# Expert rows on TensorE: none while cache pages are worked on, every fourth afterwards; gates and V rows two slots later

## The chip, the cores and the metric

The kernel runs on one core of one Trainium2 chip. The metric is device time in microseconds (us) of one execution; lower is better. The program is one launch with a fixed instruction stream for each engine (TensorE = PE, VectorE = DVE, ScalarE = ACT, GpSimd = POOL, SyncE = SP) and semaphores between them.

## What is computed

One inference step of a decoder layer for a prompt of 512 tokens and 8 sample tokens. The part that matters here is the last of the program:

```python
# 8 sequences attend over 16 cache pages of 128 tokens each
ckv_all = concatenate([cache_ckv[pages], ckv_i]); k = mla_keys(ckv_all, kpe_all, w_uk, g_k)
o = softmax(q . k) @ ckv_all @ w_uv                       # mla_sample, one sequence at a time
# expert layer, for blocks of 128 tokens, 8 heads x 16 chosen experts = 128 per token
ids, g = top-k of product keys, softmax                   # peer_ffn
act = gelu(einsum('thkd,td->thk', u_tab[ids], hb))
out = einsum('thkd,thk->td', v_tab[ids], g * act)
```

`u_tab` and `v_tab` have 16384 rows of 1024 fp32. All arithmetic is fp32.

## The kernel before

The program has a front (projections, convolution, scan, prompt attention, merge) that the change does not touch, and then `experts`, where the expert layer of the prompt, the page attention of the samples, and the rest of the samples are laid into one order of **slots**. Slot x (0 to 511 for the prompt: 4 tiles of 128 tokens, 128 slots each; 512 to 519 for the samples) stands for one chosen expert of each of 128 tokens. Each engine has its own loop `for x in range(...)` over the slots with what it does in slot x; the loops are tied by semaphores alone.

For the row of a slot the work is:
- POOL issues an indirect DMA that gathers 128 U rows (512 KB) into `u[:, x % UR]` (`UR` = 4 buffers, L2070), and an indirect DMA for the 128 V rows of slot x - BEHIND into `v[:, y % VR]` (`VR` = 8 buffers, L2077). Before each it waits until the buffer's last user is done (`u_used`, `v_used`).
- DVE multiplies and sums the U rows with the tokens' vectors (L2655), which gives one number per token in `dots`.
- Every `GS` = 4 slots ACT applies Gelu (L2386) and DVE multiplies by the gate (L2668, after waiting for `gelued`): that is the coefficient `coef`.
- Row x - LAG is added: on DVE as one `scalar_tensor_tensor` acc += v * coef (`add`, L2555; the first of a tile is L2551), or, where `by_pe(x)`, on PE: ACT makes a diagonal matrix of the coefficients (`diag`, L2394) and PE multiplies it with the V rows into `psV` (`expert_row`, L2179, four matmul records per row). `finish` adds `psV` to `acc` (L2562), multiplies by the gate of the block and adds to the residual.

Before the change `by_pe(x)` holds for every eighth slot from 62 on (x % 8 == 3): 56 rows on PE, 456 on DVE.

Into slots 62 to 435 the 128 cache pages are spread, one every 2.94 slots (`page_slot`). For a page PE transposes it (`turn`, L2148, L2149), and multiplies it with `wx` in three banks (`page_bank`, L2164, L2166); ACT copies (`page_copy`) and takes squares and sums of the keys (`page_squares`, L2377). After the 16 pages of a sequence (47 slots) a chain over DVE, ACT and PE makes the softmax and the weighted sum (`ending`, L2578 to L2602 on DVE, L2218 and L2219 on PE, slots `end` to `end` + 19). SP loads pages into 24 buffers. Buffers come free when a sequence's weighted sum is done (`weighed`). DVE also does the search for the experts of later tokens in parts between the rows (`search_part`, L1764 to L1808). From `TAIL` = slot 460 on, the samples' own projections, their expert search (slot 497 on) and their 8 expert slots follow.

The order of the work within an engine is the order of its loop. In ACT's loop, Gelu of slots 4g to 4g + 3 stands in slot 4g + 3, behind the squares of the pages of the slots before; DVE wants it in slot 4g + 5. PE does the row of slot y in its slot y + 5.

Of the kernel before, what the change touches and what calls it, by code (L numbers as in the profile page):

```python
# [19 lines left out]
ALU = mybir.AluOpType  # L20
# [10 lines left out]
TT = TP // P  # L31
# [12 lines left out]
SL = PH * TK  # L44
# [1683 lines left out]
GS = 4  # L1728
UR, VR, NPG = 4, 8, 24
LAG, BEHIND = 6, 2  # L1730
PAGE_LAG = 5
FIRST_PAGE, PAGE_SPAN = 62, 376
PE_EVERY = 8
UNITS, PARTS = TT * PH, 16
NSLOT, EXTRA = TT * SL, TK // 2
# [5 lines left out]
def after(eng, sem, n):  # L1741
    if n > 0:
        eng.wait_ge(sem, n)
# [67 lines left out]
def experts(nc, A, K, L, parts, shared, D_, outs):  # L1811


    with ExitStack() as ctx:
# [24 lines left out]
        v, u = m.sb("v", [P, VR, D]), m.sb("u", [P, UR, D])  # L1839
# [101 lines left out]
        by_pe = lambda x: x >= FIRST_PAGE and x % PE_EVERY == 3  # L1941
        on_pe = [x for x in range(NSLOT) if by_pe(x)]
        pe_index = {x: d for d, x in enumerate(on_pe)}
        last_on_pe = [max(x for x in on_pe if x // SL == t) for t in range(TT)]
        first_on_pe = [min(x for x in on_pe if x // SL == t) for t in range(TT)]
# [134 lines left out]
        def _(pe):  # L2080
# [89 lines left out]
            def expert_row(x):  # L2170
                t, r = x // SL, x % VR
                pe.wait_ge(v_in[r], 16 * (x // VR + 1))
                if x < NSLOT:
                    d = pe_index[x]
                    pe.wait_ge(diag_made, d + 1)
                    if x == first_on_pe[t]:
                        after(pe, acc_merged, t)
                    for c in range(2):
                        last = pe.matmul(psV[:, c, :], diag[:, d % 2, :], v[:, r, c * 512:(c + 1) * 512], start=(x == first_on_pe[t]),  # L2179
                                         stop=(x == last_on_pe[t]))  # L2180
# [20 lines left out]
            for x in range(XEND):  # L2201
# [25 lines left out]
                if NSLOT <= x - LAG < NSLOT + EXTRA:  # L2227
                    expert_row(x - LAG)
# [86 lines left out]
        def _(act):  # L2315
# [66 lines left out]
            for x in range(XEND):  # L2382
# [4 lines left out]
                if x - 3 >= 0 and x - 3 in pe_index:  # L2387
                    y = x - 3
                    d = pe_index[y]
                    act.wait_ge(weighted, y // GS + 1)  # L2390
                    if d >= 2:
                        o = on_pe[d - 2]
                        act.wait_ge(v_used[o % VR], o // VR + 1)
                    act.activation(diag[:, d % 2, :], K["ident"][:, :], ACT.Copy, scale=coef[:, y // SL % 2, y % SL:y % SL + 1]).then_inc(diag_made, 1)  # L2394
# [103 lines left out]
        def _(dve):  # L2498
# [58 lines left out]
            def finish(t):  # L2557
# [3 lines left out]
                dve.wait_ge(v_used[last_on_pe[t] % VR], last_on_pe[t] // VR + 1)  # L2561
                dve.tensor_tensor(acc[:, :], acc[:, :], psV[:, :, :].rearrange("p c n -> p (c n)"), ALU.add).then_inc(acc_merged, 1)  # L2562
                dve.wait_ge(acc_merged, t + 1)
# [4 lines left out]
            for x in range(XEND):  # L2568
# [92 lines left out]
                if x >= GS + 1 and (x - GS - 1) % GS == 0:  # L2661
                    g = (x - GS - 1) // GS
# [145 lines left out]
```

## Time and profile before

| | |
|---|---|
| time, three runs | 2823.23, 2823.42, 2836.57 us (median 2823.42) |
| the profiled execution's own time | 2826.46 us |
| its span, first to last instruction | 2824.8 us |
| busy in the span | PE 85%, DVE 75%, POOL 51%, ACT 33% |
| moved by DMA | 776.5 MB, mean 275 GB/s |
| granted TensorE clock, mean | 0.916 |

The span has a front of some 1069 us, the first slots to 1292 us, the stretch with the pages to about 2520 us, and the rest. A share over the whole span mixes these, so the rows below are taken from one stretch at a time. "Busy" leaves out register, semaphore and DMA-issuing instructions of SP and ACT; POOL's indirect DMA instructions count, with a gap of 0.30 us before each that is called "issue". A wait is put down to the releaser that came last. In the pages' stretch the rows of L2655 count the slots.

### The profile page before, as it was taken

The numbers are of one execution on the slowest core, as the hardware profiler recorded it, in microseconds if no ns is written. First come the engines' busy times: TensorE is split into PE (matmuls) and PEld (weight loads), VectorE is DVE, ScalarE is ACT, GpSimd is POOL, SyncE is SP. The second block draws the span as 40 slices with busy tenths as digits, with TensorE's granted clock in tenths as the row PEclk, the third lists the DMA queues.
The fourth block names the chain that finished last, engine by engine and source line by source line (L and its number), as shares of the span: only waits on it lengthen the run. The fifth ranks groups of instructions, "written<-read, shape, count | busy, mean of one in ns | idle before, by whom it ended". The sixth has DMA issues, their size and how long they took to land.

```text
span 2824.8 us, 37378 instructions
## 1 busy us (share of the span) xinstructions
PE 2394.0 (85%) x11945; PEld 1655.2 (59%) x11945; DVE 2106.2 (75%) x4074; ACT 927.2 (33%) x3628; POOL 1442.1 (51%) x1207
## 2 busy tenths in 40 slices
PE   5999997978989986887999999999999989974343
PEld 3999997864448853444565656565656546542120
DVE  3675887965555228897888978888888879897777
ACT  3431102224251112223453535444444535430110
POOL 1121332210001105776777767777778767775575
PEclk7999998989899998998999999999999999995665
DMA  6334776544006768999989999999989899999997
GB/s 196 90 80 139 212 219 151 125 129 140 12 16 211 211 223 318 399 393 388 359 282 387 361 369 351 343 362 330 391 299 397 301 372 347 356 358 357 399 337 288
DMA packets 384017, 776.51 MB, mean 275 GB/s; under 512 B 49033, under 2 KB 198618, under 8 KB 383785
## 3 DMA queue, kind: packets, MB, share of 16 engines
q0 software_dynamic: 155568, 566.17, 54.1%
q1 hardware_dynamic: 206970, 183.33, 20.8%
q10 hardware_dynamic: 21284, 24.63, 3.0%
q8 instruction: 95, 1.56, 0.2%
q14 instruction: 100, 0.82, 0.1%
HBM read 744.85 MB, written 29.37 MB: 274 GB/s over the span
## 4 chain that ended last, share of the span: by engine, by line
PE 23%; issue 12%; another core or an unknown queue 8%; DMA 8%; DVE 5%; POOL 3%; SPq 3%; ACT 1%; POOLq 0%; DVEq 0%; ACTq 0%
PE mix_pair L2164 16%; DMA mix_u<-in_peer_u,mix_ids 6%; DVE mix_acc L2555 2%; DVE mix_u L2655 2%; POOL mix_v L2077 2%; PE mix_pair L2087 2%; PE mix_pair L2179 1%; POOL mix_u L2070 1%; SPq L2027 1%; PE mix_pair L2148 1%; DMA pag_kpe<-in_cache_kpe 1%; SPq L2026 1%; PE mix_pair L2116 1%; PE mix_pair L2166 1%
## 5 line engine op out<-in xcount | busy, mean ns | idle before, releaser
L2164 PE MATMUL mix_pair<-pag_wx,pag_ckvT 128*128 128x384 f32 (+3 forms) x3072 | 972.9, 464 | 24.1 <-issue 13.5
L2077 POOL DMA_INDIRECT mix_v<-in_peer_v,mix_ids x512 | 640.2, 1250 | 225.4 <-issue 164.4
L2164 PEld LDWEIGHTS mix_pair<-pag_wx,pag_ckvT 128*128 128x128 f32 x3072 | 569.7, 193 | 315.9 <-issue 47.6
L2070 POOL DMA_INDIRECT mix_u<-in_peer_u,mix_ids x512 | 602.3, 1176 | 295.2 <-issue 144.0
L2655 DVE CUSTOM_DVE_ANT_0 mix_u<-mix_u,mix_h 128x1024 f32<-128x1024 f32 x512 | 624.2, 1219 | 165.0 <-DMA mix_u<-in_peer_u,mix_ids 142.9
L2555 DVE SCALAR_TENSOR_TENSOR mix_acc<-mix_v,mix_coef,mix_acc 128x1024 f32<-128x1024 f32 x452 | 579.5, 1282 | 0.0
L2377 ACT ACTIVATE mix_pair<-mix_pair 128x128 f32<-128x128 f32 x1024 | 270.8, 264 | 450.7 <-PE mix_pair L2164 276.4
L386 POOL CAST inp_w_hi<-inp_w 128x1024 fp32r<-128x1024 f32 x73 | 111.1, 1522 | 375.5 <-DMA inp_w<-in_w_in 296.2
L2377 ACT ACTIVATION_READ_ACCUMULATOR mix_pair<-mix_pair 128x1 f32 x1024 | 192.9, 188 | 0.0
L386 POOL CAST mrg_w_hi<-mrg_w 128x1024 fp32r<-128x1024 f32 x24 | 29.0, 1209 | 304.7 <-DMA mrg_w<-in_w_br_a 271.1
L2179 PE MATMUL mix_pair<-mix_v,mix_diag 128*128 128x512 f32 x224 | 115.3, 640 | 68.1 <-ACT mix_diag L2394 42.8
L352 PE MATMUL stp_ps<-inp_h_hi,inp_w_hi 128*128 128x260 f32 x512 | 148.3, 290 | 15.3 <-DVE inp_w_lo L346 9.6
L354 PE MATMUL stp_ps<-inp_h_hi,inp_w_lo 128*128 128x260 f32 x512 | 146.5, 286 | 0.0
L353 PE MATMUL stp_ps<-inp_h_lo,inp_w_hi 128*128 128x260 f32 x512 | 146.2, 286 | 0.0
L2365 ACT ACTIVATE pag_ckvT<-mix_pair 128x512 f32<-128x512 f32 x128 | 75.8, 592 | 149.9 <-DMA scn_ce<-keep_acs 56.7
L2386 ACT ACTIVATE mix_coef<-mix_dots 128x4 f32<-128x4 f32 x128 | 26.0, 203 | 295.4 <-DVE mix_dots L2655 257.0
L2116 PE MATMUL mix_pair<-chs_h2T,chs_wq 128*128 128x512 f32 (+2 forms) x352 | 117.2, 492 | 0.9 <-ACT chs_h2T L2349 0.6
L352 PE MATMUL cnv_ps<-inp_h_hi,inp_w_hi 128*128 128x260 f32 x400 | 116.3, 291 | 0.0
L354 PE MATMUL cnv_ps<-inp_h_hi,inp_w_lo 128*128 128x260 f32 x400 | 114.1, 285 | 0.0
L353 PE MATMUL cnv_ps<-inp_h_lo,inp_w_hi 128*128 128x260 f32 x400 | 113.9, 285 | 0.0
L2179 PEld LDWEIGHTS mix_pair<-mix_v,mix_diag 128*128 128x128 f32 x224 | 43.9, 202 | 113.2 <-issue 60.1
L352 PEld LDWEIGHTS stp_ps<-inp_h_hi,inp_w_hi 128*128 128x128 f32 x512 | 98.5, 192 | 17.0 <-issue 9.4
(532 smaller groups left out, 4328.4 us busy)
## 6 DMA issues: line engine op xcount, KB each, us to landing
inp_w<-in_w_in SPq DMA_DIRECT2D x72, 512.0 KB, 5.0
pag_ckv<-in_cache_ckv SPq DMA_DIRECT2D x88, 256.0 KB
mrg_w_ada<-in_w_ada SPq DMA_DIRECT2D x16, 1024.0 KB, 5.4
chs_wq<-in_peer_wq SPq DMA_DIRECT2D x11, 1024.0 KB
all_shared<-in_cache_ckv SPq DMA_DIRECT2D x40, 256.0 KB
keep_proj<-stp_out ACTq DMA_DIRECT2D x32, 260.0 KB
ada_w_ada<-in_w_ada SPq DMA_DIRECT2D x4, 2048.0 KB, 9.8
stp_st<-in_state_ssm POOLq DMA_DIRECT2D x8, 1024.0 KB, 7.2
```

Source lines behind the costliest of these rows:

```text
L352: pe.matmul(out, w_hi, x_hi, start=first, stop=False)
L353: pe.matmul(out, w_hi, x_lo, start=False, stop=False)
L354: return pe.matmul(out, w_lo, x_hi, start=False, stop=last)
L386: pool.tensor_copy(self.hi[:, c % 4], self.w[:, c % 2]).then_inc(self.rounded, 1)
L2070: pool.indirect_dma_start(u[:, x % UR, :], None, u_rows, bass.IndirectOffsetOnAxis(at, 0)).then_inc(u_in[x % UR], 16)
L2077: pool.indirect_dma_start(v[:, y % VR, :], None, v_rows, bass.IndirectOffsetOnAxis(at, 0)).then_inc(v_in[y % VR], 16)
L2116: last = pe.matmul(bank[2 + side][:, 0:w], wq[:, n % 2, k, side * P:(side + 1) * P], h2T[:, k, cols], start=(k == 0), stop=(k == KD - 1))
L2164: last = pe.matmul(to, ckvT[:, g % 2, k, :], wx[:, k, lo:hi], start=(k == 0), stop=(k == KL - 1))
L2179: last = pe.matmul(psV[:, c, :], diag[:, d % 2, :], v[:, r, c * 512:(c + 1) * 512], start=(x == first_on_pe[t]), stop=(x == last_on_pe[t]))
L2377: last = act.activation(psN[j][:, at:at + NOPE], psN[j][:, at:at + NOPE], ACT.Square, accum_out=ss[:, b % 2, t, h:h + 1])
L2555: dve.scalar_tensor_tensor(acc[:, :], v[:, r, :], c, acc[:, :], ALU.mult, ALU.add).then_inc(v_used[r], 1)
L2655: dve.tensor_tensor_reduce(u[:, r, :], u[:, r, :], h2[:, t % 2, :], 1.0, 0.0, ALU.mult, ALU.add, dots[:, t % 2, slot:slot + 1]).then_inc(u ...
```

## The change

Rows go to PE only from slot `end[-1]` = 440 on, the end of the pages, and there every fourth (x % 4 == 3): 18 rows (443 to 511). The 47 rows from slot 67 to 435 that PE had are DVE's. Tiles 0 to 2 then have no row on PE, so `finish` adds `psV` only for tile 3. `LAG` goes from 6 to 8 and `BEHIND` from 2 to 4: a V row is loaded two slots later and added two slots later. The gate multiplication on DVE stands in slot 4g + 7, where it stood in 4g + 5; ACT's diagonal in slot y + 5, where it stood in y + 3; PE's row in slot y + 7. The samples' rows stay at their slots on PE.

```diff
@@ constants @@
-LAG, BEHIND = 6, 2
+LAG, BEHIND = 8, 4
-PE_EVERY = 8
+PE_EVERY = 4
@@ experts @@
-        by_pe = lambda x: x >= FIRST_PAGE and x % PE_EVERY == 3
+        by_pe = lambda x: x >= end[-1] and x % PE_EVERY == 3
         on_pe = [x for x in range(NSLOT) if by_pe(x)]
         pe_index = {x: d for d, x in enumerate(on_pe)}
-        last_on_pe = [max(x for x in on_pe if x // SL == t) for t in range(TT)]
-        first_on_pe = [min(x for x in on_pe if x // SL == t) for t in range(TT)]
+        of_tile = [[x for x in on_pe if x // SL == t] for t in range(TT)]
+        merged_by = [sum(1 for rows_ in of_tile[:t] if rows_) for t in range(TT + 1)]
@@ tensor @@
-                if NSLOT <= x - LAG < NSLOT + EXTRA:
-                    expert_row(x - LAG)
+                if NSLOT <= x - LAG + 2 < NSLOT + EXTRA:
+                    expert_row(x - LAG + 2)
@@ scalar @@
-                if x - 3 >= 0 and x - 3 in pe_index:
-                    y = x - 3
+                if x - 5 >= 0 and x - 5 in pe_index:
+                    y = x - 5
@@ vector @@
-                dve.wait_ge(v_used[last_on_pe[t] % VR], last_on_pe[t] // VR + 1)
-                dve.tensor_tensor(acc[:, :], acc[:, :], psV[:, :, :].rearrange("p c n -> p (c n)"), ALU.add).then_inc(acc_merged, 1)
-                dve.wait_ge(acc_merged, t + 1)
+                if of_tile[t]:
+                    row = of_tile[t][-1]
+                    dve.wait_ge(v_used[row % VR], row // VR + 1)
+                    dve.tensor_tensor(acc[:, :], acc[:, :], psV[:, :, :].rearrange("p c n -> p (c n)"), ALU.add).then_inc(acc_merged, 1)
+                    dve.wait_ge(acc_merged, merged_by[t + 1])
-                if x >= GS + 1 and (x - GS - 1) % GS == 0:
-                    g = (x - GS - 1) // GS
+                if x >= GS + 3 and (x - GS - 3) % GS == 0:
+                    g = (x - GS - 3) // GS
```

## Rows read from the trace of the kernel before

**Rows 1.** Windows view: us, busy time and instructions by engine, PEclk, DMA share, GB/s.

```profile
1069.00:1292.00 223.00, 160.64 (x497) 87.28 (x496) 195.41 (x382) 47.98 (x97) 161.76 (x134) 0.86 1.01 384
1292.00:2520.00 1228.00, 1170.44 (x4445) 730.39 (x4444) 1032.99 (x2078) 568.78 (x2943) 901.93 (x741) 0.98 0.96 353
2520.00:2825.00 305.00, 117.80 (x454) 56.79 (x452) 233.27 (x441) 39.52 (x104) 193.32 (x163) 0.64 0.92 345
...
1145.50:1271.00 125.50, 109.33 (x354) 61.81 (x354) 115.37 (x226) 24.63 (x57) 99.35 (x80) 0.93 1.03 395
```

**Rows 2.** Chain of waits, 1327 to 1400: start, us, what.

```profile
1354.86 6.48 PE mix_pair L2164 x22
...
1362.86 6.48 PE mix_pair L2164 x22
1369.34 1.72 PE mix_pair L2179 x4
...
1372.58 6.48 PE mix_pair L2164 x22
```

**Rows 3.** Groups by line, 1292 to 2520: PE's expert rows, then DVE's.

```profile
L2179 PE MATMUL mix_pair<-mix_v,mix_diag 128*128 128x512 f32 x184 | 86.8, 594 | 0.7 <-issue 0.7
...
L2655 DVE CUSTOM_DVE_ANT_0 mix_u<-mix_u,mix_h 128x1024 f32<-128x1024 f32 x371 | 451.9, 1218 | 97.5 <-DMA mix_u<-in_peer_u,mix_ids 77.5 <-issue 18.5
L2555 DVE SCALAR_TENSOR_TENSOR mix_acc<-mix_v,mix_coef,mix_acc 128x1024 f32<-128x1024 f32 x323 | 414.2, 1282 | 0.0
...
L2668 DVE TENSOR_TENSOR mix_coef<-mix_coef,mix_gate 128x4 f32<-128x4 f32 x93 | 14.9, 161 | 69.0 <-ACT mix_coef L2386 57.4 <-issue 11.4
L2581 DVE RECIPROCAL mix_rstd<-mix_rstd 128x128 f32<-128x128 f32 x7 | 6.7, 953 | 22.9 <-ACT mix_rstd L2424 13.4 <-issue 9.5
L2562 DVE TENSOR_TENSOR mix_acc<-mix_acc,mix_pair 128x1024 f32<-128x1024 f32 x3 | 3.7, 1221 | 0.1
```

**Rows 4.** Waits of DVE, PE and POOL, 1292 to 2520: us, times, longest.

```profile
DVE mix_u L2655 <- DMA mix_u<-in_peer_u,mix_ids: 77.5, 82, 3.2
DVE mix_coef L2668 <- ACT mix_coef L2386: 57.4, 11, 8.6
DVE mix_u L2655 <- issue: 18.5, 29, 1.9
...
PE mix_pair L2148 <- DMA pag_kpe<-in_cache_kpe: 13.3, 2, 11.1
...
POOL mix_u L2070 <- DVE mix_dots L2655: 37.4, 15, 4.3
POOL mix_v L2077 <- DVE mix_acc L2555: 25.0, 4, 7.5
POOL mix_v L2077 <- PE mix_pair L2179: 21.0, 6, 13.4
```

**Rows 5.** Groups of POOL, 1292 to 2520, and last 1145.5 to 1271.

```profile
L2077 POOL DMA_INDIRECT mix_v<-in_peer_v,mix_ids x371 | 462.3, 1246 | 176.5 <-issue 119.9 <-DVE mix_acc L2555 25.0 <-PE mix_pair L2179 21.0
L2070 POOL DMA_INDIRECT mix_u<-in_peer_u,mix_ids x371 | 440.6, 1188 | 151.1 <-issue 108.7 <-DVE mix_dots L2655 37.4 <-DVE mix_acc L2551 5.1
...
L2077 POOL DMA_INDIRECT mix_v<-in_peer_v,mix_ids x40 | 60.2, 1506 | 14.3 <-issue 14.3
```

**Rows 6.** Timeline at 1158 to 1162 and at 1538: start, us, instruction, idle before.

```profile
1158.09 1.23 DVE L2655 CUSTOM_DVE_ANT_0 mix_u<-mix_u,mix_h 128x1024 f32<-128x1024 f32 x1 [0.58 <-DMA mix_u<-in_peer_u,mix_ids]
1158.28 1.85 POOL L2077 DMA_INDIRECT mix_v<-in_peer_v,mix_ids  x1 [0.30 <-issue]
...
1160.44 0.95 POOL L2070 DMA_INDIRECT mix_u<-in_peer_u,mix_ids  x1 [0.30 <-issue]
...
1161.69 1.83 POOL L2077 DMA_INDIRECT mix_v<-in_peer_v,mix_ids  x1 [0.30 <-issue]
...
1538.39 1.32 DVE L2555 SCALAR_TENSOR_TENSOR mix_acc<-mix_v,mix_coef,mix_acc 128x1024 f32<-128x1024 f32 x1
1538.45 0.95 POOL L2077 DMA_INDIRECT mix_v<-in_peer_v,mix_ids  x1 [0.30 <-issue]
```

**Rows 7.** After 2520: PE's expert rows, a DVE wait, the window 2740 to 2805.

```profile
L2179 PE MATMUL mix_pair<-mix_v,mix_diag 128*128 128x512 f32 x40 | 28.5, 851 | 67.4 <-ACT mix_diag L2394 42.8 <-DMA mix_v<-in_peer_v,mix_ids 24.6
...
DVE mix_v L1764 <- issue: 4.0, 1, 4.0
...
2740.00:2805.00 65.00, 8.91 (x10) 2.60 (x11) 55.95 (x108) 5.10 (x12) 47.02 (x42) 0.50 0.94 349
```

More of the change, by code:

```diff
@@ L2175, in expert_row @@
                     pe.wait_ge(diag_made, d + 1)
-                    if x == first_on_pe[t]:
-                        after(pe, acc_merged, t)
+                    if x == of_tile[t][0]:
+                        after(pe, acc_merged, merged_by[t])
                     for c in range(2):
-                        last = pe.matmul(psV[:, c, :], diag[:, d % 2, :], v[:, r, c * 512:(c + 1) * 512], start=(x == first_on_pe[t]),
-                                         stop=(x == last_on_pe[t]))
+                        last = pe.matmul(psV[:, c, :], diag[:, d % 2, :], v[:, r, c * 512:(c + 1) * 512], start=(x == of_tile[t][0]),
+                                         stop=(x == of_tile[t][-1]))
                 else:
```

## Prediction, made before the changed kernel was run

> **What bounds the kernel now.** I read the windows view first, to cut the span into stretches [rows 1]. The reader is to see that between 1292 and 2520 us, where the pages are, PE is busy 1170.4 of 1228 us (95%) at a granted clock of 0.98, while DVE is busy 1033.0 (84%) and DMA moves 353 GB/s. In the stretch just before it (1145.5 to 1271: no pages, no expert row on PE) DMA moves 395 GB/s and DVE is busy 92%. So with pages PE is what fills up first. After 2520 PE is nearly idle at a clock of 0.64. Second, the chain of waits inside the pages' stretch [rows 2]: from one page's block of 22 records to the next it is 8.00 us on PE, and 9.72 us where an expert row lies between, so a row costs PE 1.72 us in full. Third, the groups and waits of DVE [rows 3, 4]: of its 195 us of idle time 97.5 lie before L2655 (U rows not landed), 69.0 before the gate L2668 (Gelu late on ACT, which stands behind the squares of PE's pages), and 28.5 are the rest, of which 22.9 at the sequences' ends (L2581). Last, POOL [rows 5, 6].
>
> The stretch holds 371 rows, so a slot takes 1228 / 371 = 3.31 us. The sum is made for this stretch by DVE's time line, since DVE does every U row and releases POOL's buffers: its busy time plus its waits is the stretch's length.
>
> **The change part by part.**
>
> Rows taken from PE in the stretch: 184 records are 46 rows [rows 3], 46 x 1.72 = 79 us. PE's busy time falls to 1170.4 - 79 = 1091, with its present idle time of 57.6 us 1149 us. That is what PE would allow. It is a ceiling of the gain, 79 us, not the gain.
>
> Rows given to DVE: 46 x 1.282 us (L2555) = +59.0 us. `finish` loses three additions of `psV`, 3 x 1.22 = -3.7 us [rows 3]. The diagonals leave ACT, which has room (569 of 1228 us busy) [rows 1], at no gain. DVE's busy time becomes 1033.0 + 59.0 - 3.7 = 1088.3 us.
>
> Gates two slots later: the wait of 69.0 us has 11 cases put down to ACT, the longest 8.6 us [rows 4]. Two slots are 2 x 3.31 = 6.6 us, so at most 2.0 us of a case would be left, and PE is also less behind. With all 14 cases at that (three more are in the group's "issue" part) 28 us stay, with none 0. I take 10 us, nearer to none, because the mean case (69.0 / 14 = 4.9 us) is below 6.6. What is late next is the landing of U rows.
>
> Landings: 97.5 us now, in 111 waits (82 + 29) [rows 4]. An addition that DVE does while it would have waited costs nothing. Bounds: none of the 59.0 us hidden so, or all. By number 111 of 371 rows wait, which gives 18 us. As a wait in one slot also hides work of the slot before it, I take 27 us: 70.5 us are left.
>
> The rest of the waits, 28.5 us, is the chain at a sequence's end, where DVE, ACT and PE are tied with two slots between steps. The change leaves that, so I keep it whole.
>
> V rows issued and used two slots later: the distance from issue to use (LAG - BEHIND = 4 slots) and from use to the next issue into the same buffer stay, so 0. POOL's V row goes behind a later U row in its queue, and nothing else is on that queue. POOL no longer waits in the stretch for PE to release a V buffer (21.0 us in 6 waits, the longest 13.4 [rows 4]). That is what "unpaced" means here; its worth is inside the DVE sum, since DVE meets it as a late landing. Pages on SP keep their condition (`weighed`). PE waits 13.3 us for pages [rows 4], and if it gets there sooner that grows; PE has 1149 against the sum below, so up to some 45 us of it is hidden.
>
> Sum for the stretch: 1088.3 + 10 + 70.5 + 28.5 = 1197.3 us, against 1228: **-31 us**. PE (1149) fits below it. The nearest rows for rows without PE and pages say the same order: 40 rows in 125.5 us are 3.14 us each [rows 1, 5], with a background of other loads; 371 x 3.14 = 1165 us.
>
> After 2520: PE has 40 records = 10 rows now [rows 7], and will have the 18 of slots 443 to 511 (one of the 10 is slot 435's). DVE gives up 9 rows, 9 x 1.28 = 11.5 us, in a stretch of 305 us where it is busy 233 [rows 1]. Most of it is not DVE's to save. From 2740 to 2805 it is (56.0 of 65 us busy [rows 7]): there PE takes four rows where it had two, -2.6 us. Against it, PE does a further row ahead of the samples' scores, some 3.4 us (851 ns a record now, four records), and DVE already waits 4.0 us for these scores at L1764 [rows 7]. The end itself: the last V row waits for slot 519 of DVE where it waited for 517, but DVE's work up to there is the same sum of work minus the rows that PE takes, and PE's eight sample rows still run last. From -12 to +6 us; I take **-2 us**.
>
> Before 1292: adds start two slots later, and the same work is done by the same time: 0.
>
> In all -33 us on the profiled execution of 2826.5 us, 2793.5. Its time is 3.0 us above the median of the runs, so 2790.7, say **2791 us** on the median's scale.
>
> **A rule against the change.** POOL's V instruction takes 1.85 us when it begins under L2655 and ends 0.81 us after it, and 0.95 us otherwise [rows 6]: GpSimd is held while DVE reads two tensors. An instruction begun under L2555, which also reads two (v and acc), takes 0.95 us [rows 6]. The Trainium skill, SBUF — State Buffer, section "SBUF: two separate sides", has the shared port as an exclusive lock that a DVE instruction with two SBUF inputs takes against a GpSimd instruction that reads SBUF. For L2655 the trace agrees; for L2555 it doesn't. By the rule each of the 46 new additions would hold POOL for 0.9 us as well, 41 us in all; by the row 0.
>
> **The rivals.**
>
> Slower: **POOL's rhythm takes PE's place.** When POOL is behind, its V instruction always falls under L2655: 0.95 + 0.30 + 1.85 + 0.30 = 3.40 us a slot, which is the distance from 1158.28 to 1161.69 [rows 6]. Now POOL's mean is (462.3 + 440.6) / 371 + 0.60 = 3.03 us [rows 5], because DVE's and PE's holds let it get ahead again and its instructions then begin after L2655. If with no PE row left nothing resets it, each slot takes 3.40: 371 x 3.40 = 1261 us, +33, in all 2823 + 33 - 2 = 2854. It decides as soon as more than 6 of 10 slots run so. For it: 1145.5 to 1271 has a V mean of 1506 ns and no POOL wait but issue [rows 5]. Against it: even there a slot took 3.14.
>
> No change: **DVE takes PE's place.** The landings are set by rate and arrive later in step, none of the 59.0 us is hidden: 1088.3 + 10 + 97.5 + 28.5 = 1224 us, -4, with the end 2817. For it: DVE would be at 89% busy, and it was 92% in the densest stretch without PE rows [rows 1]. Against: 111 waits for landings are there to be filled. A bound by bytes would end here too: 353 GB/s x 1228 us = 433.5 MB. At the 395 GB/s of [rows 1] they need 1097 us and bind nothing. The Trainium skill, same page, section "A bandwidth-pool intuition that's wrong", has about 358 GB/s from HBM to a core. By that estimate the stretch couldn't fall below 1211 us, and the time below 2804; the trace's 384 and 395 speak against it.
>
> Faster yet: **all four are near 1100 and smooth each other.** The stretch runs like the one before the pages, 1165 us: -63, with the end 2758.
>
> The change might not do what it says: PE's rows may have cost it nothing since pages wait anyway. The 9.72 against 8.00 of [rows 2] excludes it.
>
> **How the numbers follow.** Forecast 2791 (its own range 2770 to 2809): 0.42. Faster yet (2758): 0.17. No change (2817): 0.24. POOL's rhythm (2854, in part 2835): 0.17. What a measurement of this kernel can tell from no change is about 0.5%, 14 us: faster is below 2809, slower above 2838. Faster 0.42 + 0.17 and a little of the third, 0.60; same 0.24; slower 0.16. The range leaves out half of the fastest case and the worse half of the slowest: 2750 to 2845.
>
> **What the changed kernel's profile would show.** In the pages' stretch: no L2179; L2555 at 1.28 us with about 46 more; PE busy near 1091 and no longer the fullest by far; DVE near 1088 of about 1197; the idle time before L2668 down from 69 to about 10; before L2655 about 70; no POOL wait for PE. If DVE's wait for landings rises above 110 with L2077's mean above 1.4 us, the slower rival holds. If the wait at L2668 stays above 40, the two slots were no cure. If PE's wait for pages passes 50 us, the step on SP's pages was wrong.

## The result

The changed kernel took **2863.6 us** (median of four runs, 2860.5 to 2874.7) beside 2830.0 us for the kernel before on the same chip: ratio **1.0132**, 95% interval 1.0084 to 1.0180. I had forecast 2791 us, with a range of 2750 to 2845. The time is slower than the forecast by 73 us and outside the range; the case "slower by over 0.5%", to which I had given 0.16, came true. Ratios, here and below, leave out executions over 1.5% above the fastest of the same kernel; medians are of all executions.

The profiled execution took 2865.5 us, its span is 2863.8 us. The stretch with the pages ends at 2549 instead of 2520 us. The windows view of after, with the columns of [rows 1]:

```profile
1292.00:2549.00 1257.00, 1121.08 (x4249) 705.78 (x4248) 1080.61 (x2122) 547.80 (x2886) 909.78 (x745) 0.94 0.93 346
2549.00:2863.00 314.00, 150.78 (x491) 64.39 (x489) 224.41 (x429) 42.45 (x118) 191.95 (x162) 0.64 0.89 332
```

The first line answers to the 1228 us of [rows 1], and holds 371 rows too. PE lost 49 us of busy time, where 79 were taken off it, and its granted clock fell from 0.98 to 0.94. DVE gained 48 us. DMA moved 346 instead of 353 GB/s. No engine is as full as PE was: PE is busy 89%, DVE 86%, and the stretch is 29 us longer. So the time is in waits, and the next views are those of DVE, whose busy time and waits make up the stretch. Groups of after by line, then DVE's waits (us, times, longest), both from 1292 to 2549:

```profile
L2657 DVE CUSTOM_DVE_ANT_0 mix_u<-mix_u,mix_h 128x1024 f32<-128x1024 f32 x371 | 450.7, 1215 | 77.7 <-DMA mix_u<-in_peer_u,mix_ids 60.0 <-issue 17.1
L2555 DVE SCALAR_TENSOR_TENSOR mix_acc<-mix_v,mix_coef,mix_acc 128x1024 f32<-128x1024 f32 x369 | 472.1, 1280 | 0.0
L2670 DVE TENSOR_TENSOR mix_coef<-mix_coef,mix_gate 128x4 f32<-128x4 f32 x93 | 14.6, 157 | 18.7 <-ACT mix_coef L2386 18.7
L2583 DVE RECIPROCAL mix_rstd<-mix_rstd 128x128 f32<-128x128 f32 x7 | 6.7, 953 | 24.9 <-ACT mix_rstd L2424 21.6 <-issue 3.3
L2077 POOL DMA_INDIRECT mix_v<-in_peer_v,mix_ids x373 | 495.4, 1328 | 144.5 <-issue 127.0 <-DVE mix_acc L2555 17.5
```

```profile
DVE mix_total L1806 <- ACT mix_exps L2433: 19.9, 4, 6.0
DVE mix_rstd L2580 <- ACT mix_raw L2379: 8.9, 1, 8.9
DVE all_o_lat L2604 <- PE mix_pair L2223: 8.5, 2, 5.3
DVE mix_rstd L2580 <- ACT mix_pair L2377: 8.0, 2, 5.5
```

(Lines moved by two: L2657, L2670, L2580, L2583 and L2604 of after are L2655, L2668, L2578, L2581 and L2602 of before.) Beside [rows 3]: landings fell from 97.5 to 77.7 us, the gate's wait from 69.0 to 18.7. What is left is 1257 - 1080.6 - 77.7 - 18.7 = **80.0 us, where there were 28.5**. It lies at the sequences' ends (L2580, L2583, L2604) and in the expert search at L1806, a line that had no such wait before: at all these places DVE stands for ACT or PE.

PE's waits in the same stretch of after:

```profile
PE mix_pair L2164 <- issue: 52.2, 19, 9.0
PE mix_pair L2164 <- ACT mix_raw L2379: 20.1, 8, 5.3
PE mix_pair L2148 <- DMA pag_kpe<-in_cache_kpe: 17.6, 4, 11.0
```

Before, the first of these was 13.5 us in 8 cases. PE does not wait for pages more (17.6 against 13.3 in [rows 4]); it stands inside a page's block.

None of the signs that I had named for the slower case shows: landings are below 110 us, the mean of L2077 is 1328 ns and below 1.4 us, the gate's wait is below 40 us, the wait for pages below 50. The time of that rival (2854) is near the measured one, its mechanism isn't what happened. That the two numbers are near is chance.

### The profile page after: what moved, and what is told of

Its sections match the earlier page's. It is cut to its first block, busy times and chain, and to the rows that moved or that the text cites. A ratio compares the mean times of both kernels' runs of the same rounds, so it can differ in the third digit from the quotient of the medians.

```text
span 2863.8 us, 37030 instructions
## 1 busy us (share of the span) xinstructions
PE 2375.3 (83%) x11793; PEld 1639.8 (57%) x11793; DVE 2147.4 (75%) x4109; ACT 909.9 (32%) x3590; POOL 1447.3 (51%) x1207
## 4 chain that ended last, share of the span: by engine, by line
PE 18%; issue 15%; DVE 10%; DMA 8%; another core or an unknown queue 4%; ACT 3%; POOL 3%; SPq 2%; POOLq 0%; DVEq 0%; ACTq 0%
PE mix_pair L2164 13%; DMA mix_u<-in_peer_u,mix_ids 5%; DVE mix_acc L2555 4%; DVE mix_u L2657 4%; POOL mix_v L2077 2%; ACT mix_pair L2377 1%; DMA all_shared<-in_peer_keys 1%; POOL mix_u L2070 1%; SPq L2027 1%; PE mix_pair L2148 1%; PE mix_pair L2087 1%; PE mix_pair L2116 1%; PE mix_pair L2250 1%; SPq L2026 1%
## 5 line engine op out<-in xcount | busy, mean ns | idle before, releaser
L2164 PE MATMUL mix_pair<-pag_wx,pag_ckvT 128*128 128x384 f32 (+3 forms) x3072 | 996.0, 473 | 81.1 <-issue 52.2
L2164 PEld LDWEIGHTS mix_pair<-pag_wx,pag_ckvT 128*128 128x128 f32 x3072 | 579.5, 197 | 381.3 <-issue 106.3
L2077 POOL DMA_INDIRECT mix_v<-in_peer_v,mix_ids x512 | 683.4, 1335 | 201.4 <-issue 173.0
L2070 POOL DMA_INDIRECT mix_u<-in_peer_u,mix_ids x512 | 564.2, 1102 | 358.8 <-DVE mix_dots L2657 165.4
L2657 DVE CUSTOM_DVE_ANT_0 mix_u<-mix_u,mix_h 128x1024 f32<-128x1024 f32 x512 | 622.9, 1217 | 161.5 <-DMA mix_u<-in_peer_u,mix_ids 140.7
L2555 DVE SCALAR_TENSOR_TENSOR mix_acc<-mix_v,mix_coef,mix_acc 128x1024 f32<-128x1024 f32 x490 | 627.2, 1280 | 0.0
L2386 ACT ACTIVATE mix_coef<-mix_dots 128x4 f32<-128x4 f32 x128 | 26.0, 203 | 379.4 <-DVE mix_dots L2657 337.5
L2179 PE MATMUL mix_pair<-mix_v,mix_diag 128*128 128x512 f32 x72 | 58.3, 956 | 77.0 <-ACT mix_diag L2394 36.3
L346 DVE TENSOR_TENSOR inp_w_lo<-inp_w,inp_w_hi 128x1024 fp32r<-128x1024 f32 x73 | 93.2, 1287 | 15.0 <-POOL inp_w_hi L386 14.6
```

What stands on the lines that cost most here:

```text
L346: dve.tensor_tensor(lo, x, hi.bitcast(F32), ALU.subtract).then_inc(lo_made, 1)
L2070: pool.indirect_dma_start(u[:, x % UR, :], None, u_rows, bass.IndirectOffsetOnAxis(at, 0)).then_inc(u_in[x % UR], 16)
L2077: pool.indirect_dma_start(v[:, y % VR, :], None, v_rows, bass.IndirectOffsetOnAxis(at, 0)).then_inc(v_in[y % VR], 16)
L2164: last = pe.matmul(to, ckvT[:, g % 2, k, :], wx[:, k, lo:hi], start=(k == 0), stop=(k == KL - 1))
L2555: dve.scalar_tensor_tensor(acc[:, :], v[:, r, :], c, acc[:, :], ALU.mult, ALU.add).then_inc(v_used[r], 1)
L2657: dve.tensor_tensor_reduce(u[:, r, :], u[:, r, :], h2[:, t % 2, :], 1.0, 0.0, ALU.mult, ALU.add, dots[:, t % 2, slot:slot + 1]).then_inc(u ...
```

## The experiments

Kernels of a group ran on one chip and share the runs of the kernel before; each ratio is to these, with its 95% interval. "Late banks" are banks of a page that PE has multiplied by its records, but of which ACT hears only microseconds later; the third set of experiments found them, and they are explained there. The stage, named below, is the time from the start of DVE's U row of slot 62 to that of slot 440 in the profiled execution: 1253 us in the kernel before (the trace of the rows above), 1284 us in after.

| group | before, median | late banks | kernel | ratio | interval |
|---|---|---|---|---|---|
| first | 2830.0 | yes | the change | 1.0132 | 1.0084 to 1.0180 |
| A | 2825.5 | yes | tail_only | 1.0014 | 0.9979 to 1.0049 |
| A | | yes | rows_only | 1.0075 | 1.0033 to 1.0117 |
| A | | yes | lag_only | 1.0087 | 1.0040 to 1.0134 |
| A | | yes | drop | 1.0101 | 1.0026 to 1.0175 |
| B | 2856.1 | yes | rows_load | 1.0230 | 1.0188 to 1.0272 |
| B | | yes | rows_paced | 1.0125 | 1.0079 to 1.0172 |
| B | | yes | gelu_late | 1.0038 | 1.0010 to 1.0065 |
| B | | yes | after_gelu | 1.0036 | 1.0002 to 1.0071 |
| C | 2764.0 | no | nowhere | 0.9943 | 0.9921 to 0.9964 |
| C | | no | dve_twice | 1.0041 | 1.0023 to 1.0060 |
| C | | no | v_late | 1.0024 | 1.0007 to 1.0041 |
| C | | no | gelu_one | 0.9986 | 0.9964 to 1.0008 |
| D | 2860.2 | yes | after_again (the change) | 1.0142 | 1.0074 to 1.0210 |
| D | | yes | rows_again (as rows_only) | 1.0112 | 1.0056 to 1.0169 |
| D | | yes | lag_again (as lag_only) | 1.0169 | 1.0112 to 1.0227 |
| D | | yes | nowhere_again (as nowhere) | 0.9986 | 0.9947 to 1.0025 |
| E | 2763.9 | no | after_third (the change) | 1.0048 | 1.0029 to 1.0066 |
| E | | no | lag_third (as lag_only) | 1.0055 | 1.0035 to 1.0074 |

### First set: the change in parts

**tail_only**: only the rows after the pages move.

```diff
-        by_pe = lambda x: x >= FIRST_PAGE and x % PE_EVERY == 3
+        by_pe = lambda x: (x >= FIRST_PAGE and x % 8 == 3) or (x >= end[-1] and x % 4 == 3)
```

(Against the kernel before. The edits of the other experiments are against the changed kernel where nothing else is said, and show the lines that matter.)

> As before, and in addition every fourth row on PE from slot 440 on, so 9 more rows on PE in the last part. All theories of the pages' stretch: within 6 us of before, 0.998 to 1.002. If the last 5 us that the changed kernel lost after slot 440 come from these rows: 1.002.

Ratio 1.0014: +4 us, with an interval from -6 to +14. My -2 us lies in it. The tail isn't where the loss is.

**rows_only**: the rows move as in the change, LAG 6 and BEHIND 2, gates, diagonals and sample rows in the slots of before.

```diff
-LAG, BEHIND = 8, 4
+LAG, BEHIND = 6, 2
...
-                if x >= GS + 3 and (x - GS - 3) % GS == 0:
+                if x >= GS + 1 and (x - GS - 1) % GS == 0:
```

> The rows are moved as in the changed kernel (none on PE while pages are there, every fourth after), but LAG, BEHIND, gates and diagonals stay as before. Theory V (VectorE took PE's place: 47 additions of 1.28 us are 60 us more for the engine that releases the buffers): as slow as the changed kernel or slower, ratio 1.010 to 1.025, since the two slots could only help. Theory C (PE has gaps without its expert rows, the granted clock falls, pages take longer): also 1.010 to 1.025, with over 150 us at half clock in the pages' stretch. Theory L (the two slots do the harm): 0.985 to 1.002.

**lag_only**: the delay as in the change, the rows on PE as before (`x >= FIRST_PAGE and x % 8 == 3`).

> The rows stay where they were before (every eighth from slot 67 on PE), and LAG, BEHIND, gates and diagonals are two slots later. Theory V and theory C: 0.985 to 1.003, the wait of DVE before the gate falls from 69 us to 20, perhaps turning up elsewhere. Theory L: 1.008 to 1.015.

Both cost: 1.0075 and 1.0087 in A, 1.0112 and 1.0169 in D. That the rows alone cost 0.75% was in none of my ranges. In rows_only DVE's wait at the gate is what grew. Its windows line of the stage and DVE's wait there (before, in its stage: 1051.25 us busy, and 58.3 us for ACT):

```profile
1278.00:2562.00 1284.00, 1141.86 (x4297) 718.31 (x4297) 1097.56 (x2156) 559.38 (x2929) 909.84 (x757) 0.94 0.93 344
```

```profile
DVE mix_coef L2670 <- ACT mix_coef L2386: 100.8, 18, 8.9
```

With the part that is called issue it is 109.1 us, and 69.9 in the kernel before. So the row part has a wait that the delay part removes, and the delay part has waits of its own; the whole is less than the two losses together (1.0132 here, 1.0142 in D).

**drop**: the changed kernel, in which DVE doesn't make its 47 new additions (the rows are loaded and released, and are missing in the result).

```diff
+                    if FIRST_PAGE <= y < end[-1] and y % 8 == 3:
+                        dve.wait_ge(v_in[y % VR], 16 * (y // VR + 1))
+                        dve.sem_inc(v_used[y % VR], 1)
-                    if not by_pe(y):
+                    elif not by_pe(y):
                         add(y)
```

> The changed kernel without the 47 additions that DVE got: the rows 67, 75 to 435 are loaded, and their buffers released, but nobody adds them (so their part of the expert sum is left out). DVE has 60 us less work, PE is as in the changed kernel. Theory V: 40 to 60 us faster than the changed kernel, 2805 to 2825, ratio 0.99 to 1.00. Theory C: only 0 to 15 us faster than it, since the pages at half clock set the pace, 2848 to 2863, ratio 1.007 to 1.013.

The windows line of its stage: DVE has 54 us less to do than in after's stage (1099.61), and the stage is as long.

```profile
1273.00:2557.00 1284.00, 1141.20 (x4297) 716.00 (x4297) 1045.26 (x2109) 558.10 (x2927) 916.19 (x759) 0.94 0.93 345
```

With late banks and the delay, DVE's additions are therefore not seen to be the cause: 1.0101 and 1.0132 can't be told apart. With late banks neither PE's time (47 rows taken off) nor DVE's (54 us taken off) buys anything that can be seen; what is left is in the waits between the engines.

### Second set: is it PE's clock, its pacing, or ACT?

**rows_load**: rows_only, with multiplications without a use on PE where its 47 rows had been; they wait for nothing of the row and nobody waits for them.

```diff
+                if FIRST_PAGE <= x - LAG + 1 < end[-1] and (x - LAG + 1) % 8 == 3:
+                    pe.wait_ge(const_in, 16)
+                    for c in range(2):
+                        pe.matmul(psV[:, c, :], K["ident"][:, :], gate2[:, c * 512:(c + 1) * 512], start=True, stop=True)
```

> The kernel with only the rows moved (LAG 6), and on PE, at the 47 places where its rows in the pages' stretch were, two multiplications of the same size (128 x 512, fp32) of constant tiles, with no wait and no reader: PE's load is back, its waits are not. Dropping 60 us of DVE work had changed nothing, so theory V is out. Theory C (clock): time at half clock in the pages' stretch falls from 167 to under 110 us, and the kernel gets as fast as before or nearly, ratio 0.997 to 1.004, though PE does 80 us more. Theory P (PE's rows paced PE to the rows, the order of the slots is lost without them): half clock stays, and 80 us more PE work cost 10 to 50 us, 1.010 to 1.025.

1.0230, the slowest of all. If all that PE lacks were work to keep its clock, filling it would have helped. The windows line of its stage:

```profile
1281.00:2623.00 1342.00, 1210.63 (x4485) 747.42 (x4485) 1097.58 (x2156) 560.67 (x2931) 901.75 (x757) 0.95 0.90 329
```

The clock went from 0.94 to 0.95 only (0.97 in the kernel before), so this run shows that refilling PE doesn't help, not what the lower clock costs. 69 us of PE's busy time came back: the rows did cost PE time, as [rows 2] says.

**rows_paced**: rows_only, with PE waiting at the place of each of its old rows for V row and diagonal, without multiplying. It tests the word "unpaced".

```diff
+                if 0 <= x - LAG + 1 < NSLOT and meets(x - LAG + 1):
+                    y = x - LAG + 1
+                    pe.wait_ge(v_in[y % VR], 16 * (y // VR + 1))
+                    pe.wait_ge(diag_made, pe_index[y] + 1)
+                    pe.sem_inc(passed, 1)
```

> The kernel with only the rows moved (LAG 6), and at the 47 places PE waits for the V row and for the diagonal, which ACT makes again, as before, but multiplies nothing: the pace is back, the load is not. Theory P: ratio 0.995 to 1.003. Theory C: 1.007 to 1.015 and over 150 us at half clock in the pages' stretch.

1.0125 beside 1.0075 and 1.0112 for rows_only and its repetition: pacing brings nothing back. The number is in the range that I had given to a falling clock, and the granted clock of the stage is 0.93. The clock's own part in the loss is not separated by any of these runs.

**gelu_late** and **after_gelu**: lag_only and the changed kernel, with ACT's Gelu two slots later, which puts it at its old distance from the gate.

```diff
-                if x % GS == GS - 1 and x < NSLOT:
-                    half, at = x // SL % 2, x % SL - (GS - 1)
-                    act.wait_ge(u_used[x % UR], x // UR + 1)
+                z = x - 2
+                if z % GS == GS - 1 and 0 <= z < NSLOT:
+                    half, at = z // SL % 2, z % SL - (GS - 1)
+                    act.wait_ge(u_used[z % UR], z // UR + 1)
```

> The kernel with the lag alone (rows as before, gates two slots later), and ACT's Gelu two slots later as well, so ACT waits for a U row that DVE has mostly done. Theory G (ACT, standing at Gelu for DVE's row, holds the copies and squares that PE's next page needs; PE stands still and its clock falls): ACT's wait before L2386 falls from about 100 us to under 30, half clock under 100 us, ratio 0.975 to 0.998. If these waits only move to the gate or to the sequences' ends: 1.003 to 1.012.

> The changed kernel with ACT's Gelu two slots later. Theory G: 0.970 to 0.995 of before, since PE's pages then run unheld and PE has 80 us less to do. Theory C alone (the clock falls for want of PE work however it is held): 1.005 to 1.013, half clock still over 150 us.

1.0038 and 1.0036: neither is faster than the kernel before, as it would be if this Gelu were what holds PE up (0.975 to 0.998 and 0.970 to 0.995). As ratios they are below lag_only (1.0087, 1.0169) and the change (1.0132, 1.0142), but these ran in other groups, and in microseconds they lie between: the medians are 2868 and 2871 us, those of lag_only and the change 2857 and 2864 in their first groups, 2893 and 2892 in D. A Gelu that ACT reaches early is a wait of ACT for DVE's row, with the copies and squares for PE's next page queued behind it: in after's stretch ACT's idle time before L2386 is 118.9 us (92.5 for L2657), in the kernel before 67.5 us. The delay had moved the gate, and left the Gelu. In the stages of gelu_late and after_gelu ACT's wait for the row is down to 3.0 and 13.5 us, and DVE's wait for ACT at the gate is back at 72.0 and 69.8 us.

### Third set: the same kernels on a chip without late banks

Group C brought a kernel before that took 2764 us, 61 to 96 us less than in the other groups, with the same program. So I compared traces of one kernel, not of two.

**nowhere**: rows_only in which the 47 rows are added by nobody (drop's edit on rows_only).

> Rows_only (distances as before, 47 rows of the stretch on DVE) with the 47 rows added by nobody: the change leaves these rows out of the result, V rows are still loaded and released. PE and DVE both have 60 to 80 us less to do than they could have. Theory A (the engines tie each other and neither PE's nor DVE's busy time sets the rate; PE's freed time becomes idle time and slower pages): ratio to before 0.998 to 1.008, like rows_only. Theory B (with the distances of before DVE's additions are in the way, as rows_load suggests): rows_only's 1.0075 less some 1.5%, 0.990 to 0.995.

> Rows of the stretch on neither engine, with the distances of before (the 47 rows are left out of the result, their V rows still loaded). It gave 0.9943 on the chip without late completions. If this chip has them: between 0.990 and 1.006, and the difference to rows_again is then what DVE's 47 additions cost; by drop against after (1.0101, 1.0132) it would be 0.3%, by nowhere against rows_only of another chip 1.3%.

Nowhere first, without, then nowhere_again, with late banks: windows line of the stage, ACT's group of squares, DVE's waits at the gate and at L2583.

```profile
1276.00:2459.00 1183.00, 1096.04 (x4297) 701.24 (x4297) 1047.14 (x2110) 556.89 (x2930) 914.29 (x755) 0.97 0.99 373
```

```profile
L2377 ACT ACTIVATE mix_pair<-mix_pair 128x128 f32<-128x128 f32 x1024 | 268.5, 262 | 292.2 <-PE mix_pair L2164 291.9
```

```profile
DVE mix_coef L2670 <- ACT mix_coef L2386: 21.3, 5, 7.8
```

```profile
1275.00:2545.00 1270.00, 1127.05 (x4297) 712.08 (x4297) 1048.09 (x2111) 561.43 (x2930) 936.62 (x758) 0.94 0.94 348
```

```profile
L2377 ACT ACTIVATE mix_pair<-mix_pair 128x128 f32<-128x128 f32 x1024 | 270.5, 264 | 437.6 <-PE mix_pair L2164 285.4 <-remote 108.4 <-issue 43.1
```

```profile
DVE mix_coef L2670 <- ACT mix_coef L2386: 69.1, 15, 7.7
DVE mix_rstd L2583 <- ACT mix_rstd L2424: 25.6, 4, 12.1
```

One program, 87 us apart in the stage. ACT waits 145 us more for PE's banks, a part of it put down to "remote" (the semaphore rose, but no instruction of PE ended near enough before it). And **the waits of DVE at the gate and at the sequences' ends go from 21 to 69 us, and from nothing to 26 us: the very waits of [rows 3] on which I had built the gain.** They are there in the kernel before with late banks (58.3 and 13.4 us for ACT in its stage, 69.9 and 22.9 with issue). Two more kernels of group C keep PE's rows, the Gelu and the gates in the slots of before, dve_twice and v_late below: DVE waits 22.1 and 17.7 us at the gate in them. So in the order of the kernel before the gate's wait is about 20 us, and it is the late banks that bring it to some 70.

What a late bank looks like, in the timeline of after from 2203 to 2233: start, length, instruction, idle time before.

```profile
2203.31 5.77 PE L2164 MATMUL mix_pair<-pag_wx,pag_ckvT 128*128 128x384 f32 x18
...
2209.33 1.60 PE L2164 MATMUL mix_pair<-pag_wx,pag_ckvT 128*128 128x264 f32 x6
...
2216.38 4.48 PE L2164 MATMUL mix_pair<-pag_wx,pag_ckvT 128*128 128x384 f32 x8 [4.90 <-issue]
2224.80 5.39 PE L2164 MATMUL mix_pair<-pag_wx,pag_ckvT 128*128 128x384 f32 x8 [3.95 <-issue]
```

```profile
2215.30 0.26 ACT L2377 ACTIVATE mix_pair<-mix_pair 128x128 f32<-128x128 f32 x1 [4.45 <-remote]
...
2223.82 0.26 ACT L2377 ACTIVATE mix_pair<-mix_pair 128x128 f32<-128x128 f32 x1 [7.59 <-remote]
...
2232.30 0.26 ACT L2377 ACTIVATE mix_pair<-mix_pair 128x128 f32<-128x128 f32 x1 [7.55 <-remote]
```

The first two lines are one page, three banks of eight records; the banks' last records end at 2206.06, 2208.64 and 2210.93. ACT squares these three banks from 2215.30, 2223.82 and 2232.30 on, each within 0.02 us of a rise of `keyed`, the semaphore that PE raises once for each bank: 9.2, 15.2 and 21.4 us after the end by the records. (Which squares belong to which bank is counted: the trace has 384 banks on either side.) PE's bank of the next page may start only when ACT has emptied the same bank of this one, so PE stands until 2216.38 and until 2224.80. Banks come 8.5 us apart, where the 22 records of a page in [rows 2] take 6.48 us.

In all, 46 waits of ACT in the trace of after end more than 1 us behind their bank's last record, with 171 us of idle time. In after_third, without late banks, there is none, and the records of the same shape follow without a gap:

```profile
2146.11 5.77 PE L2164 MATMUL mix_pair<-pag_wx,pag_ckvT 128*128 128x384 f32 x18
```

Counted so in every trace, such waits of ACT sum to 107 us in the kernel before and 108 in tail_only, which has the same order in the stage; to 188 to 199 in drop, rows_only and lag_only, which shared tail_only's group; to 167, 190, 209 and 233 in nowhere_again, lag_again, rows_again and after_again; to 205 to 230 in the four kernels of group B; and to 0 in all of C and E. So a kernel whose order in the stage is changed also meets more late banks, in the one trace that there is of each. That includes gelu_late and after_gelu (205 and 222).

**dve_twice**: the kernel before, with one operation like L2555 more on DVE at each of PE's 47 rows, which leaves `acc` as it is (the edit is against the kernel before).

```diff
+                    elif y < end[-1]:
+                        dve.wait_ge(v_used[(y - 1) % VR], (y - 1) // VR + 1)
+                        dve.scalar_tensor_tensor(acc[:, :], acc[:, :], K["ones"][:, 0:1], acc[:, :], ALU.mult, ALU.max).then_inc(again, 1)
...
```

> The kernel before with PE's rows where they are and, in the 47 slots of these rows up to 435, one scalar_tensor_tensor more on DVE over 128 x 1024 that leaves acc as it is (acc = max(acc * 1, acc)). It prices the 60 us on DVE alone. If half of DVE's additions hide in its waits for landings, as the prediction had: +30 us, 1.010. If they come on top in full, since a slot of DVE is set by the sequence U row, addition, gate: +60 us, 1.020. If DVE is not what sets the rate with PE full: 1.000 to 1.004.

1.0041, +11 us for 60 us of work: without late banks most of it hides in DVE's waits, better than I had put it. With late banks, by rows_again and nowhere_again in one group, the 47 additions cost 1.0112 - 0.9986 = 1.3%, 36 us (0.6 to 2.0% by the two intervals). (With the delay, drop beside the change had 0.3%; its interval of 1.0026 to 1.0175 leaves room for more.) Rows_load, with nearly dve_twice's work on both engines, had 1.0230 with late banks. It may be that late banks cost more the fuller both engines are; two kernels of two groups don't show it.

**v_late**: V rows two slots later, gates and diagonals in the slots of before. **gelu_one**: the kernel before with the Gelu one slot later (gelu_late's edit with 1 for 2).

> The kernel before with V rows loaded and added two slots later (8 and 4), but gates and diagonals at the slots of before. With lag_only (1.0087) it splits the delay in two. If the later gate is what costs (DVE gets further ahead of ACT and stands at the ends of the sequences): 0.998 to 1.003, and the wait before the gate stays near 60 us. If the later V rows cost by themselves (place in the queue, buffers): 1.006 to 1.011.

> The kernel before with ACT's Gelu one slot later (4g+4), the gate where it was (4g+5). If ACT standing at Gelu (67 us in the stretch before) holds up the copies and squares for PE's next page: 0.994 to 0.998, the wait at Gelu down to some 40 us. If it only moves the wait to the gate on DVE: 1.000 to 1.006, the gate's wait above 80 us.

v_late costs 0.24% (+7 us); the gates' part can't be read from lag_only of a group with late banks, but lag_third (1.0055) is without them: by it the later gates cost a further 0.3%, between two groups and hardly clear of the intervals. gelu_one can't be told from the kernel before. Its trace is the nearest that I have of the kernel before without late banks, and is used as such below.

### Fourth set: which part of the loss belongs to the late banks

Group D puts the change and its parts on one chip, and group E two of them once more.

> The changed kernel once more, to be seen beside the other three on one chip. Theory A (the loss belongs to completions of PE that reach ACT late): if this chip shows none of them (no wait of L2377 for remote), the ratio to before is 0.990 to 0.999; if it shows them, 1.009 to 1.018 with more than 100 us of these waits. Theory B (the loss belongs to the kernel's order alone): 1.009 to 1.018 either way.

> The rows alone moved (distances as before). Theory A: 0.994 to 1.000 on a chip without late completions, 1.004 to 1.012 with them. Theory B: 1.004 to 1.012 either way, since DVE's additions cost what nowhere (0.994) lacks.

> The delay alone (8 and 4, gates later, rows as before). v_late, the same without the later gates, gave 1.0024 on the chip without late completions. Theory A: 1.001 to 1.004 on such a chip, 1.005 to 1.013 with late completions. Theory B (the later gates cost by themselves): 1.005 to 1.013 either way.

D had late banks and repeats A's picture: 1.0142, 1.0112, 1.0169.

> The changed kernel on a further chip. If the chip has no late completions of PE (no wait of L2377 for remote, before near 2764 us): 0.990 to 0.999 if the loss belongs to them, 1.009 to 1.018 if it belongs to the kernel's order alone. If it has them: 1.009 to 1.018 by both.

> The delay alone on the same chip. Without late completions: 1.001 to 1.004, like v_late (1.0024), if the later gates cost only with them; 1.006 to 1.013 if they cost by themselves. With them: 1.006 to 1.018 by both.

E had none: **1.0048** for the change and 1.0055 for the delay. Neither theory had the number: without late banks the change costs 0.5%, with them 1.3 to 1.4%. So some 13 us of the loss belong to the kernel's order, and some 25 us more were seen only with late banks. Windows line, DVE's and PE's waits of after_third's stage:

```profile
1271.00:2474.00 1203.00, 1108.81 (x4297) 709.10 (x4297) 1100.57 (x2157) 555.85 (x2930) 932.12 (x758) 0.96 0.98 368
```

```profile
DVE mix_u L2657 <- DMA mix_u<-in_peer_u,mix_ids: 88.4, 119, 3.8
DVE mix_total L1806 <- ACT mix_exps L2433: 6.3, 1, 6.3
```

```profile
PE mix_pair L2148 <- DMA pag_kpe<-in_cache_kpe: 41.5, 7, 19.2
PE mix_pair L2209 <- DVE mix_diag L2591: 25.6, 7, 4.2
```

and those of gelu_one, for the kernel before:

```profile
1274.00:2464.00 1190.00, 1159.37 (x4485) 731.69 (x4485) 1051.23 (x2112) 574.92 (x2975) 922.46 (x754) 0.99 0.99 370
```

```profile
DVE mix_u L2658 <- DMA mix_u<-in_peer_u,mix_ids: 107.5, 130, 3.4
DVE mix_coef L2671 <- ACT mix_coef L2387: 20.8, 8, 5.2
```

PE's wait for pages is 41.5 us, 33.0 in gelu_one: with PE sooner at its next page it grows, as I had said, and stays below 50. From the second to the first DVE's time line changes by: busy +49.3, landings -19.1, gate -20.8 (no such wait is left), the rest (10.5 to 14.0) +3.6: +13.0 us, which is 1203 - 1190. Without late banks, by gelu_one, DVE is busy 88% of the stage already, and has 139 us to wait in, not 195. PE is busy 97% of it. What is moved from one to the other is 60 us on DVE against 51 on PE.

## Why the prediction was wrong

**The base, and with it "Gates two slots later", 69 to 10 us.** I took the waits of one trace for waits of the kernel's order, and the 59 us at the gate for a gain. 69.0 us at the gate and 22.9 at the sequences' ends stood in [rows 3]; in the same program nowhere they are 74 and 32 us with late banks, 21 and 0 without (with the part called issue), and without late banks the gate's wait is 22 and 18 us in dve_twice and v_late. Of what I meant to win at the gate, some 48 us were PE's late banks passed on through ACT. The line itself fell as I had said, to 18.7, but moving the gate doesn't bring the bank earlier: the time turned up elsewhere on DVE. This is the step that failed, and the next term is where it shows in the sum.

**The rest of the waits, "I keep it whole", 28.5 us.** Measured 80.0: the term that was mis-sized. It is 51.5 of the 59.7 us by which the stretch is longer than my 1197.3; the gate has 8.7 more than I put, the landings 7.2, and busy time 7.7 less. The gate's wait had been the place where DVE met ACT's lateness. With the gates two slots later DVE runs on and meets it at L1806 and at the ends: in after_again, with more late banks, L1806 alone has 53.7 us, in after_third 6.3. I had asked what is late next, answered "the landing of U rows", and didn't ask which other waits of DVE hang on ACT.

**Rows off PE, 79 us.** The price of a row was right in size (1.72 us in [rows 2]; rows_load got 69 us back on 47 rows of its own shape, 1.46 each). But 79 us was read as the fall of PE's busy time to 1091, and it was 1121. Without late banks PE's busy time fell by 1159.4 - 1108.8 = 51 us for 47 rows (81 us), and its granted clock from 0.99 to 0.96: by the share, about 24 us of gelu_one's stage and 96 of after_third's are at the lower level of 1.2 GHz. PE has idle time in the stage of after_third (94 us beside 31), and runs more of its work at that level. That was missing in the step: it fits the 30 us of 81 that are given back. What this lower clock costs the whole kernel isn't shown; rows_load refilled PE and lost more, but its clock rose by 0.01 only.

**Rows on DVE, +59.0 us.** Right: 1280 ns each, DVE busy 1080.6 in all against 1088.3. How much hides in the landings (27 us) was right in kind: 20 us in after, 19 without late banks. A third hidden there is too little to pay for the rest.

**V rows two slots later, 0.** Wrong by a little: v_late +0.24%, +7 us. What the trace shows of it is more waiting for U rows (116.3 us beside 107.5 in gelu_one); how the later V row does this I haven't shown.

**After 2520, -2 us.** tail_only has +4 us (-6 to +14): not refuted, of no weight.

**The rivals.** "DVE takes PE's place" comes nearest without late banks: DVE is busy 1100.6 of 1203 us, and 19 us of the additions hide in the landings, 21 where the gate's wait was. I had it at no change, since it too counted the whole gain at the gate. "POOL's rhythm" is refuted as a cause: a slot does take 1257 / 371 = 3.39 us, but POOL's own part is 1.33 + 1.12 + 0.60 = 3.05 us, hardly above the 3.03 of before, and the landings fell. Its half true part is that DVE's lateness passes to POOL: POOL's wait at L2070 for DVE is 90.5 us in after, 37.4 in [rows 4]. The rule against the change found nothing: V instructions that begin under L2555 take 0.95 us in the median in after as in before, and POOL's two groups are busy 912 us, not 41 above the 903 of [rows 5]. The bound by bytes is refuted too: nowhere moved 373 GB/s over the 1183 us of its stage. The Trainium skill, SBUF — State Buffer, section "A bandwidth-pool intuition that's wrong", with its about 358 GB/s, is below that; the measurement decides. "Faster yet" had the idea that four engines near 1100 us smooth each other at 1165 / 371 = 3.14 us a slot; drop, with less on PE and on DVE, shows the contrary with late banks (3.40). Without them nowhere has 1183 / 378 = 3.13 and after_third 3.18, so there the idea wasn't far off; what I lacked was that the kernel before, by gelu_one, is already at 3.15.

**What stays open.** Why the change suffers more from late banks than the kernel before. In medians, groups with against groups without: the kernel before +61 to +96 us, the change +88 to +116. The traces have more late waits of ACT in the change (171 and 233 us) than in the kernel before (107), but why is open. ACT standing early at its Gelu (92.5 us for DVE's row) is an explanation that I have, and the ratios of after_gelu and gelu_late fit it (1.0036 and 1.0038 with late banks), but they ran in another group than the change, the before of that group is one of the slowest, and their late waits are no fewer. I haven't shown it. The clock is the rival that no run separates: the stage of after has 0.94, that of before 0.97. The rows alone weren't run without late banks; by 1.0048 and 1.0055 they would add nothing to the delay there, as an estimate.

No kernel here beats the one before. Nowhere, which leaves work out, shows how little there was to win: with the 47 rows on neither engine 0.6% without late banks, and nothing that can be measured with them.

## What to carry to other kernels

Before a wait goes into the sum as a gain, ask who makes it: follow it back through each engine to the first that is late. If that is a matmul that reports late, or a releaser that the profile can't name, moving the waiter only moves the wait, and the same program on another chip may not have it at all. A wait between two engines is also where they are kept in step: when it is taken away, list every other wait of the same engine on the same partner, for the lateness goes there; and when a consumer is moved, move its producer's place in the queue too, or the producer stands early with other work behind it.

## What the runs showed of the hardware

**Banks of PE that are reported late.** In groups A, B, D and in the pair of the result ACT waits for banks after the end of PE's last record in them: 9.2 to 21.4 us after it in the timeline above, 22.6 us at most in after, with single waits of up to 11 us. In C and E no wait of ACT for a bank ends more than 1 us behind the bank's last record. It isn't tied to a chip for good: A and E carry the same chip's number. It isn't the kernel either, since the change, nowhere and lag_only show it in the trace of one group and not in that of the other (of the kernel before only the first trace is there, with late banks; in C and E its times alone say that they were absent). The same program was slower by 87 us of 1183 in the stage with them, by 3.6% of the whole in medians (2848 against 2750 us for nowhere). Outside the stage with the pages nothing differs: slot 62 begins at 1275.8 and 1275.1 us in the two traces of nowhere, and slots 440 to 519 take 274 and 276 us. The granted clock doesn't tell enough: it is 0.94 against 0.97 in the stage, and in 2211 to 2233, where each bank takes 8.5 us, it is 0.84 in the first half and 0.69 in the second, where eight records of 128x384 take 4.5 to 5.4 us and not 8.5. That PE only runs slower than its records doesn't explain it: after the rises of `keyed` at 2215.28 and 2223.80 three more come at 2232.28, 2232.44 and 2232.53, for three banks within 0.25 us, where one takes at least 2.6 us of PE's time (8 records of 0.32). So at least two of the completions were held back and passed on together. What holds them I can't say. In the traces with late banks a part of the events of this semaphore is missing (315 to 349, 407 in those without), so the name "remote" or "issue" says only that no releaser was found; the waits themselves are real, since ACT's and PE's own starts bound them. Every execution here was recorded by the profiler, so no run shows whether the banks would be late without it.

**The clock of PE in a paced pipeline.** Without late banks, taking 4% of its matmuls away (4485 to 4297 records) left PE at a granted clock of 0.96 instead of 0.99, a mean of the levels of 2.4 and 1.2 GHz over the stage, and its busy time fell by 51 us where the rows are 81.
